# Adding the squares of the norms on GpSimd before TensorE sums over the partitions

## What is computed

```
def rms_norm(x, g):      y = x * rsqrt(mean(x * x, -1) + EPS);  return y * g
h = modulate(rms_norm(x, norm_ffn1[l]), sh1, sc1)
x = x + 0.5 * g1 * swiglu(h, ffn1_w_in[l], ffn1_w_out[l])
```

```
x = x + mx[2] * rms_norm_2(y_x, g[1])
h = modulate_2(rms_norm_2(x, g[2]), mx[3], mx[4])        # the context: the same with y_c, ctx, mc
```

## Time and profile before

| | |
|---|---|
| median of 3 runs | 2223.14 us (2218.72 to 2224.87) |
| span of the profiled execution | 2222.6 us |
| PE busy | 2155.5 us (97%), 15539 instructions |
| VectorE (DVE) busy | 1674.6 us (75%), 2327 |
| ScalarE (ACT) busy | 990.5 us (45%), 1331 |
| GpSimd (POOL) busy | 31.1 us (1%), 33 |
| HBM read | 414.09 MB |

### The profile page before, as it was taken

How to read it: one execution, slowest core, us unless ns; L and a number is a source line. 1 busy time by engine, 2 the same in 40 slices (tenths; PEclk the granted TensorE clock), 3 DMA queues, 4 the chain that set the end, 5 groups by cost and what they waited for, 6 DMA issues and landing times.

```text
span 2222.6 us, 36384 instructions
## 1 busy us (share of the span) xinstructions
PE 2155.5 (97%) x15539; PEld 1993.2 (90%) x15539; DVE 1674.6 (75%) x2327; ACT 990.5 (45%) x1331; POOL 31.1 (1%) x33
## 2 busy tenths in 40 slices
PE   7999999999999999999999899999999999999998
PEld 7999987999999998799998678888888887889998
DVE  6999877788798877778776774777776568987563
ACT  4534434534443443443344664422222348764442
POOL 0000000000000000000000000000000001110000
PEclk9999999999999999999999999999999999999999
DMA  9999744798789864467774102254465232133662
GB/s 322 317 330 309 248 133 150 242 316 298 264 284 305 302 202 153 142 196 248 236 228 142 36 4 74 80 186 155 156 221 189 76 114 69 48 122 127 223 191 76
DMA packets 338631, 417.47 MB, mean 188 GB/s; under 512 B 9274, under 2 KB 263208, under 8 KB 338472
## 3 DMA queue, kind: packets, MB, share of 16 engines
q1 hardware_dynamic: 335360, 411.84, 56.2%
q10 hardware_dynamic: 3112, 3.33, 0.5%
HBM read 414.09 MB, written 1.05 MB: 187 GB/s over the span
## 4 chain that ended last, share of the span: by engine, by line
PE 46%; DVE 7%; ACT 3%; issue 2%; POOL 0%; DVEq 0%; ACTq 0%
PE pb L623 45%; ACT wh L1461 1%; DVE wl L2100 1%; DVE T L2108 1%; PE pb L1289 1%; DVE ACC L2108 1%; DVE SM L2694 1%; DVE RS L2192 0%; DVE Hl L2108 0%; DVE L_y L2108 0%; ACT A_P L1935 0%; DVE L_y L2100 0%; ACT L_y L1462 0%; DVE L_y L2815 0%; DVE L_u L2108 0%
## 5 line engine op out<-in xcount | busy, mean ns | idle before, releaser
L623 PE MATMUL pb<-Hh,wh 128*128 128x256 f32 (+1 forms) x2624 | 795.5, 304 | 13.8 <-DVE wl L2100 5.4
L623 PE MATMUL pb<-Hl,wh 128*128 128x256 f32 (+1 forms) x2624 | 779.3, 297 | 0.0
L623 PE MATMUL pb<-Hh,wl 128*128 128x256 f32 (+1 forms) x2624 | 774.7, 297 | 0.0
L2100 DVE TENSOR_TENSOR wl<-raw,wh 128x2048 fp32r<-128x2048 f32 (+3 forms) x271 | 600.9, 2222 | 179.9 <-ACT wh L1461 179.1
L1461 ACT ACTIVATE wh<-raw 128x2048 fp32r<-128x2048 f32 (+3 forms) x271 | 502.2, 1855 | 357.6 <-PE pb L623 259.0
L623 PEld LDWEIGHTS pb<-Hh,wh 128*128 128x128 f32 x2624 | 504.6, 192 | 33.5 <-issue 9.6
L623 PEld LDWEIGHTS pb<-Hl,wh 128*128 128x128 f32 x2624 | 504.9, 192 | 15.3 <-issue 2.2
L623 PEld LDWEIGHTS pb<-Hh,wl 128*128 128x128 f32 x2624 | 501.9, 192 | 12.8
L623 PE MATMUL pb<-Bh,wh 128*128 128x256 f32 (+1 forms) x1376 | 420.1, 305 | 7.1 <-DVE Y L2100 2.5
L623 PE MATMUL pb<-Bl,wh 128*128 128x256 f32 (+1 forms) x1376 | 413.5, 300 | 0.0
L623 PE MATMUL pb<-Bh,wl 128*128 128x256 f32 (+1 forms) x1376 | 413.4, 300 | 0.0
(11 more groups left out here) (256 smaller groups left out, 2113.9 us busy)
## 6 DMA issues: line engine op xcount, KB each, us to landing
raw<-in_ada_w_dram SPq DMA_DIRECT2D x126, 1024.0 KB, 5.5
raw<-in_ffn_w_in_dram SPq DMA_DIRECT2D x88, 1024.0 KB, 6.7
raw<-in_mlp_w_dram SPq DMA_DIRECT2D x64, 1024.0 KB, 5.3
raw<-in_ffn_w_out_dram SPq DMA_DIRECT2D x32, 1024.0 KB, 6.5
raw<-in_mix_w_in_dram SPq DMA_DIRECT2D x22, 1024.0 KB, 5.7
raw<-in_ffn_w_out_dram SPq DMA_DIRECT2D x16, 768.0 KB, 4.6
raw<-in_attn_w_qkv_dram SPq DMA_DIRECT2D x12, 1024.0 KB, 6.2
raw<-in_lru_w_in_dram SPq DMA_DIRECT2D x10, 1024.0 KB, 5.1
```

Of the source, the lines that this page charges most:

```text
L623: return e.matmul(o, l, r, start=st, stop=sp, skip_group_check=True)
L2100: return e.tensor_tensor(o, a, b, f)
```

## The change

ScalarE still squares each tile. GpSimd now adds the squares tile by tile into slot 4 of T (`add_squares`), each add waiting for the one before. In the first block (all its norms but the first) it adds tiles 1 to 5 to tile 0 (`FOLDED = 6`), and TensorE multiplies the ones with the sum, then with tiles 6 and 7. For the context's own norm and at both seams GpSimd adds all eight, and TensorE makes one multiplication per norm. At seam 1 the first four tiles of y are added 512 columns wide. The places of the sums move: see `between`. A square into a slot that still holds an older one waits for the add that reads it. The two norms of the recurrent layer, the very first norm and the last one stay as they were. Some semaphores are merged.

```diff
+FOLD_SLOT = (4, 5, 6, 7, 5, 6, 7, 5)
+FOLDED = 6
...
+            class Folded:
+                def add(self):
+                    q0, f0 = E.n["sq"], E.n["fold"]
+                    E.up("sq", 8)
+                    E.up("fold", FOLDED - 1)
+                    for i, kt in enumerate((0, *range(FOLDED, 8))):
+                        if i:
+                            E.wait_ge("sq", q0 + kt + 1)
+                        else:
+                            E.wait_ge("fold", f0 + FOLDED - 1)
+                        E.mark(mm(self.p[:, 0:self.n], ONES, T[:, FOLD_SLOT[kt], 0:self.n], i == 0, kt == 7), "fold.read")
...
+                def total(self, p, n, seg):
+                    E.wait_ge("fold", self.folded[n])
+                    E.mark(mm(p[:, SEG[seg]], ONES, T[:, 4, SEG[seg]], True, True), "fold.read")
...
-                            for kt in range(8):
-                                E.wait_ge("sq", E.up("sq"))
-                                mm(csum.p[:, 0:256], ONES, c_slot(kt), kt == 0, kt == 7).then_inc(sems["sq.read"], 1)
+                            E.up("sq", 8)
+                            E.wait_ge("fold", E.up("fold", 7))
+                            E.mark(mm(csum.p[:, 0:256], ONES, c_slot(0), True, True), "fold.read")
...
                     if c == last:
-                        sums = Sums(512 if l and seg else 256)
+                        sums = Folded(512 if l and seg else 256)
...
-                        if c == last and m:
-                            sums.add(2 * m)
...
-                        half_unit(us[1], "my", hid_at(b), 0, hid_need, said, between={(2, 2): (seam.of_x(0, 1, 2, 3),)})
-                        half_unit(us[0], "my", hid_at(b), 1, hid_need, said,
-                                  between={(1, 0): (seam.of_x(4, 5),), (1, 2): (seam.of_x(6, 7),)})
-                        half_unit(us[1], "my", hid_at(b), 1, hid_need, said,
-                                  between={(0, 2): (seam.second_x(0, 1),), (1, 1): (seam.second_x(2, 3),),
-                                           (2, 0): (seam.second_x(4, 5),), (2, 3): (seam.second_x(6, 7),)})
+                        half_unit(us[1], "my", hid_at(b), 0, hid_need, said)
+                        half_unit(us[0], "my", hid_at(b), 1, hid_need, said, between={(2, 0): (seam.of_x,)})
+                        half_unit(us[1], "my", hid_at(b), 1, hid_need, said, between={(3, 1): (seam.second_x,)})
...
-            half_unit(us[1], "o2", h_at, 0, o2_need, between={(1, 0): (seam.of_x(4, 5),)})
-            half_unit(us[0], "o2", h_at, 1, o2_need, between={(0, 5): (seam.of_x(6, 7),)})
-            half_unit(us[1], "o2", h_at, 1, o2_need,
-                      between={(0, 2): (seam.second_x(0, 1),), (0, 5): (seam.second_x(2, 3),),
-                               (1, 0): (seam.second_x(4, 5),), (1, 3): (seam.second_x(6, 7),)})
+            half_unit(us[1], "o2", h_at, 0, o2_need)
+            half_unit(us[0], "o2", h_at, 1, o2_need, between={(1, 0): (seam.of_x,)})
+            half_unit(us[1], "o2", h_at, 1, o2_need, between={(1, 6): (seam.second_x,)})
...
-                half_unit(us[1], "mf", h_at, 0, need_x, "m1.read", between={(0, 0): (seam.of_c(4, 5, 6, 7),)})
+                half_unit(us[1], "mf", h_at, 0, need_x, "m1.read", between={(0, 2): (seam.of_c,)})
...
-                half_unit(us[2], "mf", h_at, 0, need_x, "m1.read",
-                          between={(0, 0): (seam.second_c(0, 1, 2, 3),), (0, 6): (seam.second_c(4, 5, 6, 7),)})
+                half_unit(us[2], "mf", h_at, 0, need_x, "m1.read", between={(1, 0): (seam.second_c,)})
...
-                          between={0: {(1, 7): (seam.of_c(0, 1, 2, 3),)}, 1: {(0, 5): (seam.of_c(4, 5, 6, 7),)},
-                                   2: {(0, 4): (seam.second_c(0, 1, 2, 3),)}, 3: {(0, 0): (seam.second_c(4, 5, 6, 7),)}}.get(j, {}))
+                          between={1: {(0, 7): (seam.of_c,)}, 3: {(0, 2): (seam.second_c,)}}.get(j, {}))
...
+            def seam_square(kt, src, c, freed):
+                if kt == 6:
+                    act(SM[:, 25:26], KM[:, K_ONE:K_ONE + 1], ACT.Sqrt)
+                E.wait_ge("fold", freed)
+                act(T[:, FOLD_SLOT[kt], c], src, ACT.Square).then_inc(sems["sq"], 1)
...
+            def add_squares(dst, src, k):
+                E.wait_ge("sq", k)
+                E.wait_ge("fold", E.n["fold"])
+                E.mark(e.tensor_tensor(dst, dst, src, ALU.add), "fold")
```

More of the change, by code:

```diff
@@ L796, in _, with __init__ @@
             class Seam:
-                def __init__(self, sums, second):
+                def __init__(self, sums, second, adds, squares):
                     self.y, self.second = sums.p, second
                     self.root0 = E.n["rs.sqrt"] - 2
[L804 to L835, removed]
+                    f = E.n["fold"]
@@ new lines, in __init__, with of_x, second_x @@
+                    self.folded = [f := f + n for n in adds]
+                    E.up("fold", sum(adds))
+                    E.up("sq", squares)
+                def total(self, p, n, seg):
+                    E.wait_ge("fold", self.folded[n])
+                    E.mark(mm(p[:, SEG[seg]], ONES, T[:, 4, SEG[seg]], True, True), "fold.read")
+                def of_x(self):
+                    self.total(self.y, 0, 0)
+                def second_x(self):
+                    E.up("x", 16)
+                    self.p = bank(self.second, "rs.sqrt", 2)
+                    self.total(self.p, 1, 0)
@@ L837, in h_need, with of_c, second_c @@
+                def of_c(self):
+                    E.wait_ge("rs.sqrt", self.root0 + 1)
+                    self.total(self.y, 2, 1)
+                def second_c(self):
+                    E.wait_ge("rs.sqrt", self.root0 + 2)
+                    self.total(self.p, 3, 1)
+                    held[SUMS_BANK] = ("rs.sqrt", self.root0 + 3)
+                    held[self.second] = ("rs.sqrt", self.root0 + 4)
             def h_need(n=256, apart=False):
@@ L876, in ffn @@
                 mods((0, 0, l, seg), (0, 0, l, seg + 1))
-                sums.add()
+                if seg or l:
+                    sums.add()
                 if between:
@@ L1067, in mix @@
                     if m == 0:
-                        sums = Sums(256)
-                    else:
-                        sums.add(2 * m)
+                        sums = Folded(256)
                 return sums
@@ L1196, in mlp @@
                         mods(*late)
-                        seam = Seam(sums, SUMS2[1])
+                        seam = Seam(sums, SUMS2[1], (7, 7, 7, 7), 32)
                         us = [weights("m2")]
@@ L1218, in _ @@
             sums.add()
-            SQUARES["first"] = E.n["sq"]
+            SQUARES["first"] = E.n["fold.read"]
             cx_rest(between)
@@ L1542, in squares @@
                     E.wait_ge("x", E.up("x"))
-                    square(kt, XC[:, kt, 0:256], 256, gained)
+                    folded_square(kt, XC[:, kt, 0:256], 256, gained)
             cxs = [0]
@@ L1791, in f @@
                             E.wait_ge("y", E.up("y"))
-                        square(kt, Y[:, kt, SEG[seg]], 256, c0=256 * seg)
+                        seam_square(kt, Y[:, kt, SEG[seg]], SEG[seg], E.n["fold"] + kt - 3 if kt > 3 else 0)
+                    if tiles[-1] == 7:
+                        E.up("fold", 7)
                 return f
@@ L1970, in f @@
                             E.wait_ge("o2.read", E.up("o2.read"))
-                        square(kt, Y[:, kt, SEG[seg]], 256, c0=256 * seg)
+                        seam_square(kt, Y[:, kt, SEG[seg]], SEG[seg], E.n["fold"] + (kt - 3 if seg == 0 else 1 if kt == 7 else 0))
+                    if tiles[-1] == 7:
+                        E.up("fold", 4 if seg else 7)
                 return f
@@ L2903, in _, with seam_folded @@
                     barred(l, b)
+                folded(256)
+                folded(512 if l else 256)
+            def seam_folded(c, first=1):
+                skip = first if first > 1 else 0
+                q0 = E.up("sq", 8 - skip) - 8
+                for kt in range(first, 8):
+                    add_squares(T[:, 4, c], T[:, FOLD_SLOT[kt], c], q0 + kt + 1)
+            q0 = E.up("sq", 4) - 4
+            for kt in range(1, 4):
+                add_squares(T[:, 4, :], T[:, FOLD_SLOT[kt], :], q0 + kt + 1)
+            seam_folded(SEG[0], 4)
+            seam_folded(SEG[0])
+            seam_folded(SEG[1], 4)
+            seam_folded(SEG[1])
+            for seg in (0, 0, 1, 1):
+                seam_folded(SEG[seg])
             for j in range(5):
```

77 lines of the change are left out of this document (50 added, 27 removed).

## The result

The kernel after takes 2231.85 us (median of 20 runs, 2224.81 to 2241.29), the kernel before 2224.26 (20 runs, 2217.03 to 2229.71): ratio 1.0034, 95% interval 1.0022 to 1.0047. It is **7.6 us slower**, where 8.3 us faster was forecast. The profiled execution of after took 2226.46 us, near its fastest.

A forecast was written before the change was run, and what follows sets the result against it. PE's own instruction stream was taken to set the pace nearly everywhere. Terms 14.6 - 1.0 + 4.3 - 4.1 + 1.7 - 2.8 - 1.0 - 3.4 gave 8.3 us faster, 2214.8 us, range 2207 to 2222.

The forecast's parts named there:

- the sign that the prediction named itself: The prediction is wrong if the stretch from the start to 1170 us is not shorter by 11 to 15 us.
- The price of a multiplication: Everywhere on PE: one removed 256-column multiplication with ones saves 0.43 us, one of 512 columns 0.86.
- The covered norms: First block, four norms where a context unit covers the chain: all of 2.15 us gained each, 8.6 together.
- The last norm: Last norm of the first block, 512 columns: five multiplications of 0.86 us go, a gain of 4.3 us.
- The context's norm: Context's own norm: 3.0 us freed at 79 us become a longer wait at 195; adds cost VectorE something; 1.0 lost.
- The seams' x halves: Seam 1: 4.3 us gained ahead, 4.1 lost as the chain ends later; seam 2: 1.7 gained, 2.8 lost.
- The context halves: Both seams: each frees 6.0 us of PE, but chains of the same build end 0.5 us later each; 1.0 lost.
- The waits of squares for slots: Squares waiting for free slots cost nothing, since the adds they wait for are three tiles back.
- Contention: GpSimd reading SBUF and VectorE with two SBUF inputs exclude each other per instruction; adds hold seam steps 0.46 us each.
- The price of an add: GpSimd, 256 columns: 0.55 us by its size, plus 0.1 for the semaphore.
- Rival 2: A 256-column add costs hardly less than one of 512; slower from 1.1 us each, 2233 at 1.2; chance 9%.
- Clock: PE's long waits at four places bring two more half-clock losses, 3.4 us in all, ends 0 and 10 lost.

The follow-up runs named there:

- first_block: The change in the first block and context's norm only, both seams as in the kernel before: 0.9977 of the kernel before, 2219.59 us.
- before_again: The kernel before, unchanged, profiled and timed again: 0.9991 of the kernel before.
- last_alone: Kernel before with only the first block's five 256-column norms and its last, 512-column norm folded; context's norm and seams as before: 0.9948.
- context_alone: Kernel before with only the first block's five 256-column norms and the context's norm folded; last norm and seams as before: 0.9971.
- x_only: The change with the context halves of both seams multiplied by PE as before, x halves as in the change: 1.0007 of the kernel before, 2224.96 us.
- own_slots: The change with tiles 4 to 7 of the context's squares at seam 2 in slots of their own: 1.0044 of the kernel before.
- fill: The change with dummy matmuls inside PE's waits at the seams: 1.0004 of the kernel before.
- no_sum: Only the first block's five 256-column norms folded; at the seams no adds, PE multiplies the eighth square alone (unusable): 0.9908 of the kernel before, 2203.17 us.

## Why the prediction was wrong

Forecast and measurement are 15.9 us apart. By first_block 8.5 of them lie ahead of the seams (forecast 14.6 - 1.0 = 13.6, measured 5.1) and by the change against first_block 7.4 at the seams (forecast, the clock included, -5.3; measured -12.7). Each measured figure is good to some 3 us. The first part shows in the sign that the prediction named itself: the stretch up to 1170 us was to be 11 to 15 us shorter, and it is 9.1 shorter than in before, 5.6 shorter than in before_again.

**The price of a multiplication** (0.43 us) was right: three behind each other at 944.37 us, where PE waits for nothing, cost 1.29.

**The covered norms** were nearly right: 1.8 us each in the trace, not 2.15. Two low splits hold two adds each to 3.4 us, and the last of them ends at 600.71. PE starts the multiplication at 600.76, 0.39 us behind its last ordinary row in place of 0.12, so it was held for 0.27 us, a gap too short for the list of waits. This is GpSimd in the kernel after, the third norm:

```profile
592.97 3.44 POOL L2917 TENSOR_TENSOR T<-T 128x256 f32<-128x256 f32 x2 [3.24 <-ACT T L1457]
597.29 3.42 POOL L2917 TENSOR_TENSOR T<-T 128x256 f32<-128x256 f32 x2 [0.87 <-ACT T L1457]
```

"GpSimd has a whole unit for its last two adds" had no margin left. The five norms together gave 10.9 us against 10.3, but the trace has four of them some 0.35 short each, so that the fit to 10.3 is partly luck, within the noise.

**The last norm (a gain of 4.3)** failed: nothing came of it (last_alone), and in the kernel after it lost 2.8 us. Its saving was taken at 512 columns; its adds were not priced at all. They are the same adds beside the same splits, twice as wide.

**The context's norm (1.0 lost)**: right in sign, too small; it lost 2.1 us in the traces, 4.4 by context_alone. The adds run from 71.34 to 77.54 beside a row of short VectorE steps; three of them took 1.34 us before and 2.61 now, and one with a single input 0.29 before and 0.72 now, so that not only steps with two inputs are held here:

```profile
71.80 1.34 DVE L2108 SCALAR_TENSOR_TENSOR M_an<-M_kk,M_an 128x256 f32<-128x256 f32 x3
73.18 0.29 DVE L2105 TENSOR_SCALAR M_an<-M_an 128x256 f32<-128x256 f32 x1
```
```profile
71.67 2.61 DVE L2132 SCALAR_TENSOR_TENSOR M_an<-M_kk,M_an 128x256 f32<-128x256 f32 x3
74.32 0.72 DVE L2129 TENSOR_SCALAR M_an<-M_an 128x256 f32<-128x256 f32 x1
...
82.70 0.39 PE L626 MATMUL pb<-Hh,wh 128*128 128x256 f32 x1 [3.40 <-DVE wl L2124]
```

The low split comes 3 us later, and PE waits at once, at 82.70; I had looked for the wait at 195 us, where it grew only from 1.35 to 1.80.

**The seams' x halves** (4.3 - 4.1 and 1.7 - 2.8, so 0.9 lost, with the clock beside it): the chain came as described. VectorE's eight pairs of steps at seam 1 took 8.51 us (1362.96 to 1371.47) in place of 5.94, 2.6 more where 2.3 were forecast; the wait at `second_x` was 7.47 us, and the two last adds stood behind the split (3.29). But the size was too small: 2.8 us lost at seam 1 and 3.2 at seam 2; by x_only against first_block 6.7 together, with their share of the clock. At seam 1 the chain from y's last squares (10.5 us ahead of before, at 1358.46) to x's root (4.0 ahead, at 1377.20) grew by 6.5 us, not 5.0: 0.6 of the difference is the multiplication at half clock, 0.45 a slip of the prediction (by its own terms the sum would be ready at 1379.39 + 0.87 + 2.3 + 2.3 + 1.2 = 1386.1, not 1385.6), and the rest fits dearer adds (below). The dummies at half clock then held PE for another 1.7. Seam 2 was not taken apart in this way.

**The context halves (1.0 lost together) are where the mechanism failed.** They lost 2.0 us at seam 1 and 4.5 at seam 2 in the traces, and 6.0 together by x_only, again with their share of the clock. The step said that chains "of the same build" grow by what PE is freed of. They don't: at seam 2 seven adds, not two, stand behind the split, because the squares start only just ahead of it (before too, at 1795.60, with VectorE's split at 1797.92: it could have been read there), and each late sum holds PE, whose lateness holds ScalarE's next high split. The x half's pattern was carried over, and the adds were never laid against VectorE's timeline. The waits of squares for slots, costed at nothing, do exist (3.21 us), but own_slots shows that taking them away gains nothing.

**Contention** was taken as a term of the adds. It is more: 53 adds that nobody reads cost 9.6 us. **The price of an add** was 0.55 us and 0.1 for the semaphore; alone it is 0.72 to 0.74 (1.29 for 512 columns), and in series one starts 0.87 behind the other (the six at 1805.70), 0.22 more than the 0.65 of the prediction. The 0.72 is above the estimate of 0.56 from the Trainium skill (GPSIMD Engine Reference, Elementwise: side-by-side cycle accounting). Rival 2 came nearest in time, and in part by luck: its price of 1.1 us is the mean duration in the trace (1106 ns for 256 columns), but most of what is above 0.72 comes from holding, not from size.

**Clock (3.4)**: fill makes it 3 us by the two profiles and 7 by the medians, within the ends given.

## What to carry over

An engine that is idle is not free: here GpSimd's adds held VectorE's steps (0.48 becoming 0.95 us), so before work is moved there, lay it against VectorE's timeline at each place, and move only what falls where VectorE has gaps and PE is not soon to wait for it. Where the chain of other engines sets the time, removed matmuls are worth only what lies ahead of the chain; leaving the work out altogether (no_sum) measures that ceiling in one run. One norm's accounting doesn't carry over to another that looks alike: price each, the narrow and the wide, the covered and the one in the chain.

## What the runs showed beside

- The times of one kernel go with its granted clock. Of the 20 runs of the change, those with a mean clock of 0.982 took 2224.8 to 2228.6 us, those with 0.974 to 0.977 took 2233.3 to 2241.3.
- Half clock falls differently in two executions of the same kernel. Before and before_again have spans of 2222.6 and 2215.8 us; from 1232 to 1242 they show (columns of the earlier trace rows):

```profile
1232.00:1242.00 10.00, 5.94 (x41) 3.33 (x40) 7.36 (x21) 4.03 (x13) 0.00 (x0) 1.00 0.00 1
```
```profile
1232.00:1242.00 10.00, 8.62 (x58) 6.02 (x58) 7.09 (x17) 5.06 (x16) 0.00 (x0) 0.66 0.01 2
```

  A difference of 2 us between two single profiles in one stretch can be this alone.
- What decides whether a wait of 3.4 us brings half clock (1156 us in the change) or none (the same wait in last_alone) stays open.
